# Six matmuls of 256 columns in place of two of 512 and two of 256, and results read straight from PSUM

## The reference

```python
h = rmsnorm(x, g_mix);  proj = h @ w_in          # q, k, v, forget logits, lru x, lru gate, memory q, merge gates
y_fox = forgetting_attention(...)                # 8 heads of 128, QK norm, causal
y_lru = rg_lru(conv4(lx), ...) * gelu(lg)        # width 1024
y_mem = memory_attention(...)                    # 4 heads of 256 over 256 memory tokens
y_d = einsum('bsnc,ncd->bsnd', [y_fox, y_lru, y_mem], w_branch)
x = x + sum(sigmoid(gate_logits + b_gate) * y_d) @ w_out
up = conv3(rmsnorm(x, g_ffn) @ w_ffn_up)         # 2 x 5632
return x + (gelu(up_act) * up_val) @ w_ffn_down
```

## Time and profile before

| | us |
|---|---|
| median of 3 runs | 1662.53 (1662.39 to 1663.37) |
| profiled execution, span from first to last instruction | 1661.6 |
| TensorE busy | 1641.6 (99%), 9356 matmuls |
| weight loads busy | 1426.6 (86%) |
| VectorE busy | 1117.1 (67%) |
| ScalarE busy | 895.9 (54%) |
| GpSimd busy | 54.9 (3%) |
| from HBM | 304.69 MB, 185 GB/s over the span |

### The profile page before, as it was taken

The page is one execution under the profiler, slowest core; times in us unless marked ns, Lnnn a source line. Parts: engine busy times, 40 slices in busy tenths (PEclk is TensorE's granted clock), DMA queues, the critical chain, the costliest instruction groups (busy, mean ns, idle before and its releaser), DMA issues.

```text
span 1661.6 us, 27207 instructions
## 1 busy us (share of the span) xinstructions
PE 1641.6 (99%) x9356; PEld 1426.6 (86%) x9356; DVE 1117.1 (67%) x1324; ACT 895.9 (54%) x1145; POOL 54.9 (3%) x57
## 2 busy tenths in 40 slices
PE   7999999999999999999999999999999999999998
PEld 6888888888888888888888888888888888888887
DVE  6977677678847566575666777777777777544443
ACT  6766567466644544545455555555555555434332
POOL 0010112000000000000001000000000000000000
PEclk9999999999999999999999999999999999999999
DMA  8544456553555555555565555555555655655653
GB/s 301 195 151 162 150 172 200 188 167 126 177 185 185 191 187 190 189 189 190 177 192 189 176 190 200 189 179 189 192 178 185 202 189 186 201 197 196 202 195 102
DMA packets 85833, 307.37 MB, mean 185 GB/s; under 512 B 9944, under 2 KB 11232, under 8 KB 85664
## 3 DMA queue, kind: packets, MB, share of 16 engines
q1 hardware_dynamic: 84672, 302.89, 55.0%
q0 software_dynamic: 1120, 3.94, 0.8%
HBM read 304.69 MB, written 2.11 MB: 185 GB/s over the span
## 4 chain that ended last, share of the span: by engine, by line
PE 94%; DVE 2%; issue 2%; ACT 1%; DMA 1%; SPq 0%; POOL 0%; ACTq 0%; DVEq 0%; POOLq 0%
PE psG L315 91%; PE psM L315 2%; DVE fox_rstd L910 1%; DVE W L885 1%; DMA mem_raw<-memT 0%; ACT W L554 0%; DMA lru_rg<-w_rg 0%; PE psM L406 0%; ACT fox_rstd L593 0%; DVE fox_S L938 0%; DVE stat L941 0%; DVE fox_q_n L926 0%; ACT L554 0%; ACT fox_S L583 0%; ACT fox_S L605 0%
## 5 line engine op out<-in xcount | busy, mean ns | idle before, releaser
L315 PE MATMUL psG<-X,W 128*128 128x512 f32 (+1 forms) x5632 | 993.2, 338 | 0.0
L315 PEld LDWEIGHTS psG<-X,W 128*128 128x128 f32 x5632 | 860.4, 188 | 128.1 <-issue 2.4
L885 DVE TENSOR_TENSOR W<-raw,W 128x1024 fp32r<-128x1024 f32 x567 | 687.8, 1227 | 314.9 <-ACT W L554 312.2
L554 ACT ACTIVATE W<-raw 128x1024 fp32r<-128x1024 f32 x567 | 591.2, 1054 | 318.7 <-PE psG L315 314.6
L315 PE MATMUL psG<-hidden,W 128*128 128x512 f32 (+1 forms) x1408 | 245.4, 337 | 0.0
L315 PEld LDWEIGHTS psG<-hidden,W 128*128 128x128 f32 x1408 | 214.0, 188 | 31.3
L562 ACT ACTIVATE low<-psG 128x512 f32<-128x512 f32 x140 | 83.8, 598 | 224.6 <-PE psG L315 224.6
L315 PE MATMUL psG<-Y,W 128*128 x768 | 134.4, 337 | 0.0
L315 PEld LDWEIGHTS psG<-Y,W 128*128 128x128 f32 x768 | 117.0, 188 | 17.1
L1300 DVE SCALAR_TENSOR_TENSOR up_c<-up_pad,par_sb,up_c 128x256 f32<-128x256 f32 x176 | 77.5, 482 | 42.3 <-ACT up_c L829 36.3
L315 PE MATMUL psG<-merged,W 128*128 128x512 f32 (+1 forms) x512 | 89.3, 337 | 0.0
(11 more groups left out here) (185 smaller groups left out, 672.5 us busy)
## 6 DMA issues: line engine op xcount, KB each, us to landing
raw<-w_units SPq DMA_DIRECT2D x567, 512.0 KB, 3.4
xs<-xT SPq DMA_DIRECT2D x4, 512.0 KB, 9.8
outT<-xs POOLq DMA_DIRECT2D x7, 256.0 KB, 3.6
mem_raw<-memT SPq DMA_DIRECT2D x3, 512.0 KB, 9.0
lru_rg<-w_rg POOLq DMA_DIRECT2D x8, 128.0 KB, 4.3
c_all<-c_rows POOLq DMA_DIRECT2D x1, 1024.0 KB, 8.8
mem_raw<-memT SPq DMA_DIRECT2D x4, 128.0 KB, 2.5
raw<-w_units SPq DMA_DIRECT2D x2, 256.0 KB, 3.2
```

What stands on the lines that cost most here:

```text
L315: return nc.tensor.matmul(*a, skip_group_check=True, **kw)
L554: nc.scalar.activation(W[:, s, :, 0], raw[:, s], ACT.Copy).then_inc(hi_done, 1)
L885: V.tensor_tensor(W[:, s, :, 1], raw[:, s], f32(W[:, s, :, 0]), ALU.subtract).then_inc(lo_done, 1)
```

## The change

All matmuls of the weight stream move 256 columns. For a k-tile and for each of the three products in turn (high x high, high weights x low operand, low weights x high operand) the two channel halves are multiplied, and all six add into one bank, half t into columns 256t to 256t + 255. A group now fills one bank with its finished result, and psG has two banks in place of four. `low`, `yd`, `copy_low` and `add_low` are gone. The result is read from PSUM by its user, on the engine given by `EMPTIED_BY` (a ScalarE, d VectorE, one letter per w); `emptied` counts how many groups an engine has emptied by then, and TensorE, before filling a bank, waits for that count of the group that used it last.

```diff
+EMPTIED_BY = {"mv": "aa", "mkq": "da", "lru": "aa", "v": "aa", "qk": "aa", "gate": "aa", "branch": "dd",
+              "out": "dd", "up": "dd", "down": "dddd"}
@@ TensorE, group
-                b = 2 * (w % 2)
-                g = G0[phase] + w
-                if i is not None or g >= 2:
-                    pe.wait_ge(evac_done, at(g - 1, i, NG[phase]) + before[1])
+                if free_act is not None:
+                    pe.wait_ge(emptied_act, free_act)
+                if free_dve is not None:
+                    pe.wait_ge(emptied_dve, free_dve)
...
-                        halves = [slice(t * P, t * P + P) for t in range(2)]
-                        for t, ts in enumerate(halves):
-                            if rows_major:
-                                mm(psG[:, b + t, :], x_hl[:, 0, ts], W[:, s, k], start=kt == 0, stop=False)
-                            else:
-                                mm(psG[:, b + t, :], W[:, s, k, 0, ts], x_hl, start=kt == 0, stop=False)
-                        for t, ts in enumerate(halves):
-                            if rows_major:
-                                ins = mm(psG[:, b + t, T:], x_hl[:, 1, ts], W[:, s, k, 0], start=False, stop=kt == last)
-                            else:
-                                ins = mm(psG[:, b + t, T:], W[:, s, k, 1, ts], x_hl[:, 0], start=False, stop=kt == last)
+                        for w_part, x_part in ((0, 0), (0, 1), (1, 0)):
+                            for t in range(2):
+                                ts = slice(t * P, t * P + P)
+                                dst = bank_tiles(w)[:, t]
+                                begin = kt == 0 and w_part == 0 and x_part == 0 and t == 0
+                                end = kt == last and w_part == 1
+                                if rows_major:
+                                    ins = mm(dst, x_hl[:, x_part, ts], W[:, s, k, w_part], start=begin, stop=end)
+                                else:
+                                    ins = mm(dst, W[:, s, k, w_part, ts], x_hl[:, x_part], start=begin, stop=end)
@@ ScalarE
-            def copy_low(g, last, i=None, coef=8, groups=2):
+            def empty(last, dst, w, i=None, coef=8):
                 act.wait_ge(pe_units, at(last + 1, i, coef))
-                if g >= 2:
-                    act.wait_ge(evac_done, at(g - 1, i, groups))
-                b = 2 * (g % 2)
-                nc.scalar.activation(low[:, g % 2], psG[:, b:b + 2, T:], ACT.Copy).then_inc(low_copied, 1)
+                nc.scalar.activation(dst, bank_tiles(w), ACT.Copy).then_inc(emptied_act, 1)
@@ ScalarE, iteration
-                    if k in (7, 11):
-                        copy_low(G0[phase] + k // 11, U0[phase] + k - 4, i)
+                    if k == 7 and kind == "lru":
+                        act.wait_ge(lru_taps, i * 3)
+                    if k == 11 and kind == "lru":
+                        wait(dve=side_count("lru", i - 1, "dve", "gelu"))
+                    if k == 7 and kind == "fox" or k == 11 and kind == "mem":
+                        wait(dve=side_count(kind, i - 1, "dve", "normed"))
+                    if k == 11 or k == 7 and kind != "mem":
+                        empty(U0[phase] + k - 4, destination(phase, 0, k // 11), k // 11, i)
@@ VectorE, quarter: the branch product is multiplied straight from the bank
-                            add_low(G0["gate0"] + n, yd[:], q, groups=QUARTER_GROUPS)
-                            dve.wait_ge(evac_done, at(G0["gate0"] + n + 1, q, QUARTER_GROUPS))
-                            dve.wait_ge(gate_ready, q * 6 + (2 * i + w + 1))
+                            filled(QUARTER0 + k - 4, q, QUARTER_UNITS)
+                            dve.wait_ge(emptied_act, emptied("gate0", i, w) + q * 6)
                             dst = acc[:, w] if i == 0 else gates[:, i, w]
-                            V.scalar_tensor_tensor(dst, gates[:, i, w], 1.0, yd[:], ALU.add, ALU.mult).then_inc(gated, 1)
+                            V.scalar_tensor_tensor(dst, gates[:, i, w], 1.0, bank_tiles(w), ALU.add, ALU.mult
+                                                   ).then_inc(emptied_dve, 1)
@@ VectorE, up_scale
-                dve.wait_ge(evac_done, at(G0["up"] + w + 1, i, 2))
-                V.tensor_tensor(up_pad[w][:, :, 2:], up_pad[w][:, :, 2:], rstd2.rearrange("p (a t) -> p a t", a=1).to_broadcast([P, 2, T]),
-                                ALU.mult).then_inc(up_scaled, 1)
+                filled(U0["up"] + 4 * w + 3, i)
+                V.tensor_tensor(up_pad[w][:, :, 2:], bank_tiles(w), rstd2.rearrange("p (a t) -> p a t", a=1).to_broadcast([P, 2, T]),
+                                ALU.mult).then_inc(emptied_dve, 1)
@@ VectorE, down (out is alike)
-                        add_low(g, yd[:], i, groups=4)
-                        dve.wait_ge(evac_done, at(g + 1, i, 4))
+                        filled(U0["down"] + k - 4, i, 4 * per)
                         tiles = xs[:, bass.ds(i * 8 + 2 * w, 2)]
-                        V.tensor_tensor(tiles, yd[:], tiles, ALU.add).then_inc(out_done, 1)
+                        V.tensor_tensor(tiles, bank_tiles(w), tiles, ALU.add).then_inc(emptied_dve, 1)
```

More of the change, by code:

```diff
@@ L256, in f32, with bank, bank_tiles @@
             return ap.bitcast(F32)
+        def bank(w):
+            return psG[:, w % 2]
+        def bank_tiles(w):
+            return bank(w).rearrange("p (a t) -> p a t", a=2)
         QUARTER0, QUARTER_UNITS = U0["gate0"], U0["gate1"] - U0["gate0"]
@@ L473, in plain, with plain_first @@
             def plain(phase, i, hooks, operand=x_op, **kw):
                 for w in range(2):
-                    group(phase, i, w, operand, hooks, **kw)
-            mkq(None, {7: mem_sums})
+                    group(phase, i, w, operand, hooks, free_act=emptied(phase, i - 1, w), **kw)
+            def plain_first(phase, hooks, frees, operand=x_op, **kw):
+                for w in range(2):
+                    group(phase, None, w, operand, hooks, **frees[w], **kw)
+            mkq(None, {7: mem_sums}, {"free_act": emptied("mv", 1, 0)})
@@ L484, in _ @@
             with pe.Fori(1, 2) as i:
                 plain("v", i, decay_hooks(), rows_major=True)
-            plain("qk", None, {})
+            plain_first("qk", {}, [{"free_act": emptied("v", 1, w)} for w in range(2)])
             with pe.Fori(1, 4) as i:
                 plain("qk", i, attention_hooks("fox", i - 1))
-            plain("gate0", None, attention_hooks("fox", 3))
+            plain_first("gate0", attention_hooks("fox", 3), [{"free_act": emptied("qk", 3, w)} for w in range(2)])
@@ L492, in quarter @@
             def quarter(q, first_gate):
-                before = (q * QUARTER_UNITS, q * QUARTER_GROUPS)
+                units_before = q * QUARTER_UNITS
+                act_before, dve_before = q * 6, q * 6
                 with pe.Fori(first_gate, 3) as i:
-                    plain("gate0", i, {}, before=before)
+                    for w in range(2):
+                        group("gate0", i, w, x_op, {}, units_before=units_before,
+                              free_act=emptied("gate0", i - 1, w) + act_before,
+                              free_dve=emptied("branch0", -1, w) + dve_before)
@@ L508, in _ @@
             with pe.Fori(0, 4) as i:
-                plain("out", i, {}, operand=lambda kt: merged[:, kt], ready=lambda n: pe.wait_ge(merged_lo, 2 * n + 2))
+                for w in range(2):
+                    group("out", i, w, lambda kt: merged[:, kt], {}, ready=lambda n: pe.wait_ge(merged_lo, 2 * n + 2),
+                          free_dve=emptied("out", i - 1, w))
             def x2_sums():
@@ L516, in x2_sums @@
                 ins.then_inc(x2_ss, 1)
-            plain("up", None, {3: x2_sums}, ready=lambda n: pe.wait_ge(h2_lo, 2 * n + 2))
+            plain_first("up", {3: x2_sums}, [{"free_dve": emptied("out", 3, w)} for w in range(2)],
+                        ready=lambda n: pe.wait_ge(h2_lo, 2 * n + 2))
             with pe.Fori(1, FT // 2) as i:
-                plain("up", i, {})
+                for w in range(2):
+                    group("up", i, w, x_op, {}, free_dve=emptied("up", i - 1, w))
             with pe.Fori(0, 2) as i:
@@ L782, in quarter @@
                         kind, i, w, n = group
-                        copy_low(G0["gate0"] + n, QUARTER0 + k - 4, q, coef=QUARTER_UNITS, groups=QUARTER_GROUPS)
+                        if kind == "gate":
+                            act.wait_ge(pe_units, at(QUARTER0 + k - 3, q, QUARTER_UNITS))
+                            if not first and i == 0:
+                                act.wait_ge(acc_added, q * 4)
+                            for t in range(2):
+                                ins = nc.scalar.activation(gates[:, i, w, t], bank_tiles(w)[:, t], ACT.Tanh, scale=0.5,
+                                                           bias=half_bg[:, bass.ds(q * 4 + (i * KT + 2 * w + t), 1)])
```

(18 more changed lines are left out.)

157 lines of the change are left out of this document (72 added, 85 removed).

## The result

The changed kernel takes **1713.99 us** (median of 4 runs, 1713.19 to 1715.38) against 1662.83 for the kernel before on the same chip (1662.39 to 1663.37): ratio 1.0306, 95% interval 1.0291 to 1.0320. It is slower by 51.2 us where 13.9 us of gain were forecast. The profiled span grew from 1661.6 to 1713.7, by 52.1 us, and the two traces say where.

What follows compares the result with a forecast made beforehand. The prediction took TensorE's long queue of stream matmuls as the bound: 1661.6 (profiled span) + 0.9 (to the median) - 11.1 (stream) - 1.4 (tail) - 1.4 (fox heads) = 1648.6 us, range 1628 to 1690.

Steps and rivals of the forecast that it cites:

- What bounds the kernel: Whole kernel: TensorE, busy 99%, is one long matmul queue; the 568 units of the weight stream take 1583 us.
- The distance between 256-column matmuls: Weight stream: 115.3 ns each, six per k-tile 691.8 ns against 696.7, -11.1 us; the forecast had chance 0.48.
- fixed cost: Rival, weight stream: each matmul has a fixed part, 6.1 ns give or take 3, shifted into the 512s' distances; 1687.4 us, chance 0.20.
- Columns alone: Rival, weight stream: only columns count, 0.4536 ns each, so no change to be told; 1659.7 us, chance 0.18.
- Supply at 0.12: Rival, TensorE's sequencer: supply falls behind without 512s, 0.12 us a matmul, +53 us, some 1713; chance 0.09.
- The load is the pace: Rival, weight stream: weight loads set the distance at 0.111 us, the stream loses 70 us, 1590; chance 0.05.
- The emptying: Results leaving PSUM: copies and additions dropped, mostly hidden under TensorE; unhidden gains in tail and fox heads, -1.4 us each.
- the tail: After the last matmul: one VectorE addition of 0.69 us remains of a copy and two additions, -1.4 us.
- the fox heads: TensorE's waits for softmax weights, 1.7 us in three places, shorten as ScalarE takes over VectorE's addition for q; -1.4 us.
- q's bank: Fox heads: ScalarE, ahead of emptying q, waits for the previous head's norms, from 353.34 to 355.66; claimed hidden.
- The prediction's own mark: Weight stream: the prediction is wrong if a unit is outside 2.75 to 2.78 us, or TensorE waits for a bank.
- evenly: Sign of the fixed-cost rival: psG chain pieces at 117 to 118 ns per matmul, evenly.

Runs made afterwards that it cites:

- e1: The kernel before with only the width changed: each 512-column matmul made as two of 256, emptying as before; 1715.87 us against 1663.08, ratio 1.0317.
- the series: Two sets of 64-matmul series added behind the changed kernel's last group, by width, order, weights and type; 120.0 ns for 256 fp32r columns, 109.2 in bfloat16.
- s1: The changed kernel with twelve series of 64 matmuls added behind its last group, into spare banks; fp32r distances 226.7 ns for 512 columns, 120.0 for 256.
- v3: As v2, with a unit's matmuls sorted by type, eight fp32r and then sixteen bfloat16; 1647.54 us against 1663.16 for the kernel before, ratio 0.9909.
- e5: The changed kernel with TensorE's loop of the down projection written out twice, no jump back; 1709.77 us, 4.2 us less than the changed kernel.
- e2: The changed kernel with the matmuls and four banks of before, small products left out of results; 1659.6 us, ratio 0.9979 to the kernel before.
- v1: The changed kernel with both small products in bfloat16, weight copy on ScalarE, down loop written out; 1685.22 us against 1663.48 for the kernel before.
- v2: As v1, but VectorE makes the bfloat16 copy of the weights in place of ScalarE; 1671.11 us, ratio 1.0046 to the kernel before.
- e3: The kernel before with a k-tile's matmuls in the order 512, 256, 512, 256; 1665.94 us, ratio 1.0021.

## Why the prediction was wrong, and where it was right

**What bounds the kernel: right.** TensorE's stream is the whole path, the loads lie under it, and a change of the pace reaches the end undiminished: e1 alone gives the 52 us.

**The distance between 256-column matmuls: the step that failed.** The prediction took the 115.3 that a 256 shows in pairs between 512s and wrote it for six in a row. In a row they stand at 120.0, six make 720.0 and not 691.8, and over 2272 k-tiles that is +52.9 where -11.1 stood. The reading of the earlier trace rows was exact: the series give the same 233 and 112 to 119 in that order. What was wrong is to take a distance in a mixture as the price of its member. A pair of 512s and 256s is the unit that was measured, and 696.7 is four fixed parts of 13.3 and 640.0 of columns, 693.3, and 3.4 for the changes of width. Two matmuls more, less the changes: 2 x 13.33 - 3.4 = 23.3 ns a k-tile. The prediction had the sign of this in hand: "The 512 costs slightly more than two 256s, which I can't explain". One width alone can't cost more than its two halves if each start costs something, so the remark spoke for a part that passes between neighbours, and weighed against the sum, not for it.

**The rival "fixed cost": the right mechanism, mis-sized.** It had 6.1 ns, give or take 3, from f32 matmuls, and a time of 1687. Plain f32 makes two instructions of each product (64 written in s1, 128 recorded); with 256 columns they follow each other at 215.8 ns, the same as 512 columns of bfloat16. If each of them passes its columns twice, its part is the small one, 2.5; no run here shows the two passes. The rows were the nearest, but of another type, and the bound was drawn as narrow as if they were of the same; the range's upper end, 1690, was this rival's and too low with it. The earlier trace rows were put against this rival, though an order of two widths can't tell it from the forecast.

**Columns alone: wrong.** 0.4536 ns a column would be 116.1; 120.0 was measured. Its argument, that the earlier trace rows have the same mean with 40-column weights, does not hold without the mixture: at 256 columns the series give 120.0, 116.0, 116.7 and 113.4 for weights of 128, 96, 64 and 32 columns.

**Supply at 0.12: its number came, its mechanism did not.** 1713 was its price, for a stream paced by the sequencer, and that 1714 was measured is chance. 111.7 at 128 columns, 109.2 in bfloat16 and 113.1 over the 6240 pairs of v3 rule that out. Of the supply only one thing was real, the 4 us at the jump, and no step of the prediction had it: it belongs to the longer loop body (e5), and the trace of before had shown the jump for 0.225 us.

**The load is the pace: wrong.** Pairs of load and matmul follow each other at 111.7 with 128 columns and with 64 (s1), close to the 0.111 of the earlier trace rows, so something other than the columns bounds the small sizes. Load and supply are not told apart there; neither bounds the 256.

**The emptying: right in size.** -2.8 was forecast for the tail and the fox heads; e2 measures -3.5 [-5.2, -2.0]. The tail is -1.4 to the digit. The fox heads, forecast at -1.4, gave 2.0 in e2 and 2.7 in the changed kernel, but e1, which empties as before, has 2.2 there: at the slower stream the wait would have gone without the new emptying. TensorE waits for no bank, and q's bank is emptied by ScalarE behind the norms without anyone waiting, as forecast: it had stood 4.08 us idle for them.

```profile
364.81 0.60 ACT L605 ACTIVATE fox_q_raw<-psG 128x512 f32<-128x512 f32 x1 [4.08 <-DVE fox_q_n L972]
```

ScalarE is busy 844 and not 830, VectorE 1033 and not 1020, neither on the path. The prediction's own mark, a unit outside 2.75 to 2.78, said at first sight that it was wrong (2.880), and of its signs the one that fitted best was that of the fixed cost, "evenly", with 120.0 in place of 117 to 118.

## What to carry to other kernels

A distance read inside a mixture is the price of the mixture: before an operation is multiplied, find it, or measure it, in a row of its own kind. A matmul that is split costs its columns and one more fixed part, and that part depends on the type (13.3 ns in fp32r with 128 weight columns, 2.5 in bfloat16), so wide matmuls matter most where it is large. When instructions are added to a long loop, look at its jump.

## What was not expected of the hardware

- The fixed part of an fp32r matmul is 13.3 ns at 256, 320, 384 and 512 columns, and smaller with narrower weights: at 256 columns 9.3 with 96, 10.0 with 64, 6.7 with 32. With 128 columns and with 64 it is 111.7 between starts, so that the columns no longer decide. Why fp32r has it stays open.
- Neighbours of another width or type shift each other's distances: a 512 beside 256s stands at 228 to 241 and not 226.7, a 256 beside 512s mostly at 113 to 117 and not 120. In no order run here is the sum less than that of the parts: +3.4 ns for each k-tile of the kernel before, +13 to 14 for each k-tile that changes type and back (v1, v2). The order 512, 256 has two paces in executions of one kernel (e3).
- A loop body of 1056 pairs pays 4 us when it jumps back and has its instructions brought again; one of 704 pays nothing that can be seen and has none brought.
- In the series of 64-column matmuls of s1 the distance was 111 to 112 for 28 of them and then 213 to 215. There the granted clock was at the lower of its two levels (1.2 of 2.4 GHz), 0.53 as the mean of the stretch shown. Before it fell, the engine had run matmuls of 128 columns and then of 64, back to back. The rows: length of the stretch, busy times of the five engines, granted clock, DMA share, GB/s.

```profile
1764.20:1767.00 2.80, 2.80 (x28) 2.80 (x27) 0.00 (x0) 0.00 (x0) 0.00 (x0) 1.00 0.00 0
1767.50:1774.00 6.50, 6.50 (x34) 6.50 (x34) 0.00 (x0) 0.00 (x0) 0.00 (x0) 0.53 0.01 3
```

This touches the reading of the series behind it, those of weights with 64 columns: their first matmuls fall into the low clock, and the 116.7 is taken from the later ones at the full one.
